# State inputs behind the scores, stick values in pairs, GpSimd for seven more weight low halves, and rope tables in four steps, in a two-block fp32 kernel

## The reference, cut to what matters

```
# first block
u = rmsnorm(x, norm_mix);  u_ssm, q, k, v = split(u @ w_in, [512, 1024, 1536])
y_ssm = s5_branch(u_ssm, ...)      # per group: x_t = Abar x_{t-1} + Bbar u_t,  y_t = Re(C x_t) + D u_t
                                   # then gelu, and y * sigmoid(y @ w_glu + b_glu)
y_attn = stick_breaking(q, k, v)   # 8 heads of 64: z = q k / 8, masked to s < t
                                   # w = exp(log_sigmoid(z) + sum over s<j<t of log_sigmoid(-z_j));  w @ v
g_ssm, g_attn = split(sigmoid(u @ w_gate + b_gate), 2)
merged = g_ssm * (y_ssm @ w_up_ssm) + g_attn * (y_attn @ w_up_attn)
h = h + merged @ w_out
hid = relu(rmsnorm(h, norm_mlp) @ w_ff1);  h = h + (hid * hid) @ w_ff2
# second block: two layers of convolutions and latent attention, modulated by ada = silu(c) @ w_ada + b_ada
cos, sin = cos/sin(positions * inv_freq)   # the rope tables, the same for both layers
```

## Time and profile before

| | busy us | share | instructions |
|---|---|---|---|
| profiled execution | 1071.31, span 1069.6, mean granted PE clock 0.981 | | 19601 |
| PE | 1020.7 | 95% | 8132 |
| DVE | 696.7 | 65% | 1052 |
| ACT | 545.7 | 51% | 631 |
| POOL | 376.4 | 35% | 159 |
| DMA | 177.22 MB by SP's queue | 52.0% | |
| median of the runs without the profiler | 1069.53 | | |

### The profile page before, as it was taken

How to read it: one execution, slowest core, us unless ns; L and a number is a source line. 1 busy time by engine, 2 the same in 40 slices (tenths; PEclk the granted TensorE clock), 3 DMA queues, 4 the chain that set the end, 5 groups by cost and what they waited for, 6 DMA issues and landing times.

```text
span 1069.6 us, 19601 instructions
## 1 busy us (share of the span) xinstructions
PE 1020.7 (95%) x8132; PEld 960.3 (90%) x8132; DVE 696.7 (65%) x1052; ACT 545.7 (51%) x631; POOL 376.4 (35%) x159
## 2 busy tenths in 40 slices
PE   7998999889999999999999999999999999999996
PEld 6985777779899999989999999999789999999995
DVE  4958788773435322345977986856449789877563
ACT  5455554744544444446654744644366456446442
POOL 3079673003487888710056530000100456300000
PEclk8998999999999999999999999999899999999998
DMA  8642444664774656553744555554556444564601
GB/s 278 197 159 81 157 157 159 222 212 158 242 231 126 194 193 187 186 175 123 237 129 148 161 175 178 160 195 158 153 163 203 153 130 150 182 192 147 209 19 40
DMA packets 159496, 179.58 MB, mean 168 GB/s; under 512 B 5040, under 2 KB 141744, under 8 KB 159408
## 3 DMA queue, kind: packets, MB, share of 16 engines
q1 hardware_dynamic: 159024, 177.22, 52.0%
q0 software_dynamic: 384, 1.10, 0.3%
HBM read 177.26 MB, written 1.05 MB: 167 GB/s over the span
## 4 chain that ended last, share of the span: by engine, by line
PE 76%; DVE 9%; issue 7%; ACT 5%; DMA 2%; POOL 1%; SPq 0%; DVEq 0%; ACTq 0%; POOLq 0%
PE pg L1791 64%; DVE p_bu L1669 2%; ACT w_hi L924 2%; PE p_s L1874 2%; DVE area L1243 2%; PE p_y L1949 1%; ACT u_hi L899 1%; PE pg L1812 1%; PE p_s L1767 1%; DVE area L1261 1%; PE p_s L1928 1%; DVE rows L1285 1%; DVE area L1247 1%; DMA area<-in_c_state 1%; PE p_bu L1928 1%
## 5 line engine op out<-in xcount | busy, mean ns | idle before, releaser
L814 POOL TENSOR_TENSOR w_lo<-raw,w_hi 128x2048 fp32r<-128x2048 f32 x61 | 285.3, 4688 | 316.9 <-ACT w_hi L924 316.9
L924 ACT ACTIVATE w_hi<-raw 128x2048 fp32r<-128x2048 f32 (+3 forms) x153 | 275.1, 1804 | 67.5 <-PE pg L1791 29.3
L1234 DVE TENSOR_TENSOR w_lo<-raw,w_hi 128x2048 fp32r<-128x2048 f32 (+2 forms) x92 | 190.7, 2084 | 61.0 <-ACT w_hi L924 60.8
L1791 PE MATMUL pg<-u_hi,w_hi 128*128 128x256 f32 x1536 | 213.5, 291 | 16.7 <-ACT u_hi L899 11.0
L1791 PEld LDWEIGHTS pg<-u_hi,w_hi 128*128 128x128 f32 x1536 | 195.9, 193 | 27.2 <-issue 11.4
L1791 PE MATMUL pg<-u_lo,w_hi 128*128 128x256 f32 x1536 | 202.9, 285 | 0.0
L1791 PE MATMUL pg<-u_hi,w_lo 128*128 128x256 f32 x1536 | 200.2, 283 | 0.0
L1791 PEld LDWEIGHTS pg<-u_lo,w_hi 128*128 128x128 f32 x1536 | 194.3, 195 | 0.0
L1791 PEld LDWEIGHTS pg<-u_hi,w_lo 128*128 128x128 f32 x1536 | 191.4, 192 | 0.0
L930 ACT ACTIVATE area<-pg 128x512 f32<-128x512 f32 (+1 forms) x92 | 54.1, 588 | 155.5 <-PE pg L1791 143.6
L1669 DVE SCALAR_TENSOR_TENSOR p_bu<-area,par,p_bu 128x256 f32<-128x256 f32 x232 | 93.9, 483 | 0.8
(11 more groups left out here) (221 smaller groups left out, 1343.6 us busy)
## 6 DMA issues: line engine op xcount, KB each, us to landing
raw<-in_w_in SPq DMA_DIRECT2D x68, 1024.0 KB, 5.4
raw<-in_w_ff SPq DMA_DIRECT2D x32, 1024.0 KB, 5.6
raw<-in_w_ada SPq DMA_DIRECT2D x24, 1024.0 KB, 5.3
raw<-in_w_gate SPq DMA_DIRECT2D x8, 1024.0 KB, 7.8
raw<-in_w_o SPq DMA_DIRECT2D x8, 1024.0 KB, 5.2
raw<-in_w_out SPq DMA_DIRECT2D x4, 1024.0 KB, 8.7
raw<-in_w_b_out SPq DMA_DIRECT2D x4, 1024.0 KB, 5.1
raw<-in_w_c_out SPq DMA_DIRECT2D x4, 1024.0 KB, 5.5
```

Source lines behind the costliest of these rows:

```text
L814: pool.tensor_tensor(w_lo[:, s, 0:n], raw[:, r, 0:n], w_hi[:, s, 0:n].bitcast(F32), ALU.subtract).then_inc(sem(f"raw_free{r}"), 1)
L924: act.activation(dst, src, ACT.Copy).then_inc(*(c.event("w_hi", q["s"]) if i == len(parts) - 1 else c.step()))
L1234: ins = dve.tensor_tensor(dst, src, hi.bitcast(F32), ALU.subtract)
L1791: ins = pe.matmul(pg[g % 2][0:m, i * T:i * T + T], w[:, k, a:a + m], x[:, k, :], start=x is x_hi and w is wh and (i, k) == turns[0], stop= ...
```

## The change

Five edits.

1. On PE `bu` of pair 2m+1 is issued behind `stick_scores` of head m+1, no longer between and ahead of its two matmuls.
2. The weighted values of the stick heads are issued for two heads at once (`weighted_pair`), behind `s5_out` in rounds 2, 4 and 6, and for the last two after the loop as before. DVE's `stick_weights` now waits for the pair of head m-2. ACT's copy of the pair stands ahead of its take of the ada panel.
3. `high_ahead` (ACT's `w_hi` of up_attn 1) stands ahead of S5's gelu instead of behind its first half.
4. `POOL_LOW` also has up_attn 0 and 1, up_ssm 0 and 1, out 0 and 1, and glu 0: seven low halves go from DVE to GpSimd.
5. The rope tables are four steps, after ff1 panels 4, 5, 6 and 7, and `modulate_columns` stands after chunk 4. SP's order of DMAs is the same.

```diff
-POOL_LOW = [("gate", n) for n in range(3, 8)] + [(job, n) for job in ("ff1", "ff2") for n in range(2 * DFF // W)]
+POOL_LOW = [("gate", n) for n in range(3, 8)] + [(job, n) for job in ("up_attn", "up_ssm", "out") for n in range(2)] + [("glu", 0)] + [(job, n) for job in ("ff1", "ff2") for n in range(2 * DFF // W)]
...
             step("stick_scores", m + 1)
-        else:
-            step("bu", 2 * m + 1)
+        step("bu", 2 * m + 1)
...
+        if m and m % 2 == 0:
+            step("stick_out", m - 2)
         ada_panel(m + 1)
...
-        if m:
-            step("stick_out", m - 1)
-    step("stick_out", HEADS - 1)
+    step("stick_out", HEADS - 2)
     step("ada_turn", 10)
     step("s5_out", HEADS - 1)
     step("split", "ctx")
+    step("high_ahead", count["split"] + 2)
     step("s5_y", WT - 1)
     step("s5_gelu")
     step("table_set", "sigmoid_and_others")
-    step("high_ahead", count["split"] + 2)
...
                 panel("ff1", 0, 2 * c + n, "w_ff1", 0, W * c + 256 * n, KT, 256, 1)
+                if c in (2, 3):
+                    step(("rope_angles", "rope_reduced", "rope_half", "rope_tables")[2 * c - 4 + n])
...
-        if c == 2:
-            step("rope_tables")
+        if c == 4:
             step("modulate_columns", 0)
...
             def stick_weights(hd, _):
...
-                    dve.wait_ge(sem("o_stick"), over("o_stick", hd - 2))
+                    dve.wait_ge(sem("o_stick"), over("o_stick", (hd - 2) // 2))
...
+            def rope_reduced(_, __):
+                rows = slice(NOPE, P)
                 turns(nmean[rows], sin_cos[rows], cos_sin[rows])
+
+            def rope_half(_, __):
+                rows = slice(NOPE, P)
                 ts(nmean[rows], sin_cos[rows], 0.5, None, ALU.mult).then_inc(*c.event("rope_angle"))
+
+            def rope_tables(_, __):
+                rows = slice(NOPE, P)
                 dve.wait_ge(sem("rope_sines"), over("rope_sines"))
...
             def stick_out(hd, _):
-                pe.wait_ge(sem("w_stick"), over("w_stick", hd))
+                pe.wait_ge(sem("w_stick"), over("w_stick", hd + 1))
...
-                weighted_values(v1, stick_w[:, hd % 2], hd).then_inc(*event("o_stick", hd))
+                weighted_pair(v1, stick_w, hd).then_inc(*event("o_stick", hd // 2))
```

More of the change, by code:

```diff
@@ L1138, in stick_out @@
             def stick_out(hd, _):
[L1139 to L1144, removed]
+                i = hd // 2
+                act.wait_ge(sem("o_stick"), over("o_stick", i))
+                fn(context1[:, i, :], p_o[:, T * (i % 2):T * (i % 2) + T], ACT.Copy).then_inc(*c.event("ctx", i))
+            def rope_half(_, __):
                 act.wait_ge(sem("rope_angle"), over("rope_angle"))
@@ L1210, in _ @@
                          stick_scores=stick_scores, stick_weights=stick_weights, stick_out=stick_out,
-                         rope_tables=rope_tables, prescale=prescale, latent_sums=latent_sums,
+                         rope_half=rope_half, prescale=prescale, latent_sums=latent_sums,
                          latent_roots=latent_roots, scores=scores, turn=turn, ln_a_squares=ln_a_squares, ln_a_var=ln_a_var,
@@ L1593, in gate_take, with rope_angles @@
                     take(g, bconv[:, 2 * n:2 * n + 2, :], both, bconv[:, 2 * n:2 * n + 2, :], ALU.mult)
-            def rope_tables(_, __):
+            def rope_angles(_, __):
                 for pad in (apad[:, :, 0:CONV_A - 1], bpad[:, :, 0:CONV_B - 1]):
@@ L1751, in _ @@
                          stick_scores=stick_scores, stick_soft=stick_soft, stick_weights=stick_weights,
-                         ada_end=ada_end, glu_mul=glu_mul, gate_take=gate_take, modulate=modulate, rope_tables=rope_tables, u2_piece=u2_piece, modulate_columns=modulate_columns,
+                         ada_end=ada_end, glu_mul=glu_mul, gate_take=gate_take, modulate=modulate, rope_angles=rope_angles, rope_reduced=rope_reduced, rope_half=rope_half, rope_tables=rope_tables, u2_piece=u2_piece, modulate_columns=modulate_columns,
                          latent_norm=latent_norm, rope_k=rope_k, rope_q=rope_q, conv_a=conv_a, conv_b=conv_b, scores=scores,
@@ L1915, in s5_turn, with bu @@
                 ins.then_inc(*event("bt_ps"))
-            def bu_ready(r):
+            def bu(r, _):
                 pe.wait_ge(sem("bt"), over("bt", 1))
@@ L1924, in bu_ready @@
                     pe.wait_ge(sem("root"), over("root", ("norm", 0)))
-            def bu_part(r, comp):
                 f, rows = r // FOUR, slice(32 * (r % FOUR), 32 * (r % FOUR) + 32)
[L1928 to L1934, removed]
+                bank_ = (p_bu, p_s)[r % 2]
+                for comp in range(2):
+                    ins = pe.matmul(bank_[:, T * comp:T * comp + T], bt[rows, comp, f, :], ussm[rows, f, :],
+                                    start=True, stop=True)
+                ins.then_inc(*event("bu", r))
             def s5_out(j, _):
@@ L1958, in stick_scores @@
                 rows, f = slice(64 * (hd % 2), 64 * (hd % 2) + 64), hd // 2
-                if hd:
-                    bu_ready(2 * hd - 1)
-                    bu_part(2 * hd - 1, 0)
                 pe.matmul(p_z[:, 0:T], k1[rows, f, 0:P], q1[rows, f, :], start=True, stop=True)
-                if hd:
-                    bu_part(2 * hd - 1, 1).then_inc(*event("bu", 2 * hd - 1))
                 pe.matmul(p_z[:, T:T + P], k1[rows, f, P:T], q1[rows, f, P:T], start=True, stop=True).then_inc(*event("z", hd))
@@ L1988, in weighted_pair @@
                 return ins
[L1990 to L1994, removed]
             def stick_out(hd, _):
-                pe.wait_ge(sem("w_stick"), over("w_stick", hd))
+                pe.wait_ge(sem("w_stick"), over("w_stick", hd + 1))
                 for s, v in emptied(groups_of("v")):
                     pe.wait_ge(s, v)
-                if hd >= 2:
+                if hd:
                     pe.wait_ge(sem("ctx"), over("ctx", hd // 2 - 1))
-                weighted_values(v1, stick_w[:, hd % 2], hd).then_inc(*event("o_stick", hd))
+                weighted_pair(v1, stick_w, hd).then_inc(*event("o_stick", hd // 2))
             def latent_stats(l, _):
```

## The result

The changed kernel takes 1093.2 us, the median of four runs (1090.83 to 1096.57), against 1069.05 before: a ratio of 1.0231 (95% interval 1.0197 to 1.0265). It is slower, clear of noise; whether by 2% or more, the interval just leaves open. Beside the later experiments it took 1092.33 against 1069.27, 1.0222 (1.0198 to 1.0247). Its profiled execution took 1094.54 us, where the sum had 1094.9.

A forecast was written before the change was run, and what follows sets the result against it. PE, with 76% of the chain of waits, was taken to bound the kernel; -5.1 + 5.3 + 20.0 + 3.4 = +23.6 on 1071.3 gave 1094.9 profiled, 1093 by the median; own range 1083 to 1101, wider range 1070 to 1101.

The forecast's parts named there:

- A: Chunks 2 and 3: only one of the two chains of standing rope steps forms; +10, 1080 us; chance 0.16.
- B: Chunks 2 and 3: the rope steps meet no GpSimd low half, 64 rows being too short; -1.8, 1068 us; chance 0.11.
- C: Up section: DVE and GpSimd share rather than shut out, so it gains 8.2; -15, 1054 us; chance 0.11.
- D: Loop: pairs do not lie side by side or the order brings nothing; 0 for edits 1 and 2; 1098 us; chance 0.04.
- Forecast waits 10.2 and 11.8: Two PE waits in us at ff2 takes, behind ff1 panel 5 and panels 6 and 7; less 1.95 gained, +20.0.
- The clock's term: Chunks 2 and 3: PE's clock drops behind each ten us wait, 1.7 us taken twice; +3.4, bounds 0 and +7.
- +5.3: Up section, edits 3 and 4: glu 3.2 later, up_ssm 1 gets 2.4 back, out 0 loses 4.5; bounds -8.2 and +16.
- The term that was laid wrong: Out 0 loses 4.5 us: `u_lo` stands behind one GpSimd low half, the take before it behind another.
- The first step, at up_attn 0: Up_attn 0's last pass comes 2.0 us later, because GpSimd's low half takes 4.6 where DVE's took 2.3.
- The bound from below, -8.2: Up section: DVE's seven low halves only vanish and nothing stands, so PE's waits and the clock dip go; -8.2 us.
- -6.9: Loop, lower bound for edits 1 and 2: the slow round of 15.96 us also gets its 1.75 us of clock back.
- -5.1: Loop, edits 1 and 2: -2.7 for `bu` behind the scores and -2.4 for pairing the weighted values.

The follow-up runs named there:

- the experiment with one low half: Edits 1 to 3, rope steps ahead of the feed-forward section, angles behind out 0; added: up_ssm 1's low half on GpSimd. 1060.77 us, 0.9919 of the kernel before.

## Why the prediction was right

*What decides.* The reading of the earlier trace rows, that DVE and GpSimd shut each other out and that a waiting GpSimd gets in between two DVE steps, is shown by the trace after (9.82 and 4.54 us), by edit 5 alone and, with the five low halves beside the rope steps moved from GpSimd to DVE and the order of the rope steps kept, by 1.33 and 0.42. Rivals A, B and C fall with it. D falls by edits 1 and 2 alone, at least 6.3 us shorter.

*Edit 5.* Forecast waits 10.2 and 11.8, found 9.39 and 10.85. The chains ran as laid out, step for step: two scalar steps free, the first and second `scalar_tensor_tensor` behind one low half each, then `va_lo`, the last `scalar_tensor_tensor` and one scalar step. They came out 0.8 and 0.95 smaller. Most of the first is that two low halves, the steps slipping between them, take 9.19 us, where 9.8 had been laid (324.93 to 334.7). The clock's term was 3.4 and is 4.4: the ff2 panel behind each wait took 7.6 and 8.4 us instead of 5.76, so the dip behind a ten us wait costs 1.8 and 2.6, more than the 1.7 behind one of 2.44.

*Edits 3 and 4.* +5.3 was too small; +7.3 came. In its parts: up_attn 1 started 0.8 late (0.9 was said), glu 2.1 (3.2), up_ssm 1 won 1.6 (2.4), and out 0 lost 6.8 where 4.5 was said: 1.3 until it starts, 5.5 within it. The term that was laid wrong is the last. It was not `u_lo` that stood (1.49 for two, as always), nor the take before it (0.69, as its own reading of the earlier trace rows should have said), but the additions to the merged rows, at 222.72, 226.86 and 235.01. With them PE waited 2.97 ahead of the panel and 3.70 within it (1.61 and 0.93 before), and its clock fell to the lower level, 0.52 from 236 to 245: 3.62 us for sixteen matmuls that take 2.08. Of the 5.5 within the panel half is waiting and half the clock, and no clock term had been laid there. The first step, at up_attn 0, was right in size but not in cause: its last pass came 1.8 later because PE waited 1.55 for `va_lo`, which stood for GpSimd, not for the slower low half of the weights. The bound from below, -8.2, treated DVE's gain as real; the experiment with one low half shows that it mostly isn't, since DVE's next low half waits for it.

*Edits 1 and 2.* PE's own work was sized rightly for edit 1 (0.39 a round, 0.38 said) and 0.2 a single head too low for edit 2. The slow round with its 1.75 us, which the bound calls that of rows 5, is that of the earlier trace rows. The clock of the middle rounds, put into the bound (-6.9) and not into the sum, came: no profile of a kernel with both edits, seven in all, has a slow round after the second, while the four of kernels with neither have one or two each (edit 1 alone none, edit 2 alone one). The medians give the loop 9.7, beyond the bound, but with an interval that holds it. By the profiles alone, -6.8 stands against -5.1, of which 1.7 is the slow round at full clock again.

So the mechanisms were right, and the closeness of the total is luck: the loop and the waits came out 1.7 smaller each than their terms, the up section and the clock 2.0 and 1.0 larger, and 1094.5 against 1094.9 is what is left. One more thing in the chances doesn't hold: the range from 1070 leaves out rival B's own 1068 as well as C, and the two have 0.22 between them, not some 0.15.

## What to carry to other kernels

Before moving work from VectorE to GpSimd to relieve it, list VectorE's steps that run beside it. If they read two SBUF operands, or are scalar steps within SBUF, a move that spares VectorE 2.3 us can cost it up to the 4.6 us of GpSimd's instruction, each time that one of them is issued beside it. A chain of short dependent steps was the worst neighbour of long GpSimd instructions here, since a link of 0.3 or 0.4 us could pay for one whole instruction of 4.6; put such a chain where GpSimd has nothing, even far from where its result is used. There the steps kept their own lengths, though what that won over edits 1 to 3 was too little for the times to show.

## What the runs showed of the hardware

A scalar step of 32x256 elements, 0.3 us alone, stood for a GpSimd instruction (4.79 us for two) as the two-input steps of 128 rows did. GpSimd's own low halves grew where DVE worked with two SBUF inputs in the up section: 10.12 us and 10.15 for two at 188 and 202 us, against 9.19 for the two beside the three `scalar_tensor_tensor` of 64 rows.

The loop's first two rounds took 28.2 to 33.8 us in the thirteen profiles of the twelve kernels, and the edits don't explain the order. Every one of them has a stretch at the clock's lower level there, and when it comes makes the difference. In four profiles (before, the changed kernel twice, edit 1 alone) the clock was whole until PE waited 2.25 us for DVE ahead of the second round, and fell behind that wait: 32.6 to 33.8 us. In the other nine it fell earlier, PE came later and that wait was 0.8 us or none: 28.2 to 32.0. The spread is twice what edit 1 is worth, and one profile of each kernel can't tell such parts apart there.
